# Output weights and mixed tiles loaded beside a recurrence's tail, and its sums and scales moved from VectorE to ScalarE

## The reference

```python
p = einsum('btd,de->bte', rmsnorm(x, norm_mix), w_in)          # 3584 columns: groups A, B, C
oa = stick_breaking_attention(...)                             # 4 heads x 64
ob = chunk_band_attention(...)                                 # 4 heads x 64
oc = hgrn2_scan(S0, q_c, k_c, v_c, log_f, block)               # 4 heads x 128, a gated linear recurrence
oc = rmsnorm(oc, onorm_c).reshape(B, T, W_C) * silu(gc)
mixed = concatenate([oa, ob, oc], axis=-1)                     # 1024 columns
h = x + einsum('bte,ed->btd', mixed, w_o)
u = relu(einsum('btd,df->btf', rmsnorm(h, norm_ffn), w_up))    # 4096 columns
return h + einsum('btf,fd->btd', u * u, w_down)
```

## Time and profile before

| what | us |
|---|---|
| median of 3 runs (lowest, highest) | 3034.61 (3033.84, 3037.02) |
| the profiled execution | 3033.76 |
| its span | 3031.6 |
| TensorE busy in the span | 2923.2 (96%) |
| VectorE busy | 1647.0 (54%) |
| ScalarE busy | 959.6 (32%) |
| GpSimd busy | 327.8 (11%) |

### The profile page before, as it was taken

The page is one execution under the profiler, slowest core; times in us unless marked ns, Lnnn a source line. Parts: engine busy times, 40 slices in busy tenths (PEclk is TensorE's granted clock), DMA queues, the critical chain, the costliest instruction groups (busy, mean ns, idle before and its releaser), DMA issues.

```text
span 3031.6 us, 45479 instructions
## 1 busy us (share of the span) xinstructions
PE 2923.2 (96%) x18136; PEld 2590.6 (85%) x18136; DVE 1647.0 (54%) x2293; ACT 959.6 (32%) x1639; POOL 327.8 (11%) x504
## 2 busy tenths in 40 slices
PE   7999899899999999759999999999999999999999
PEld 5788788888888999748999999889999997888887
DVE  5554454476666578843544454535444545355554
ACT  3331366455555222122222222222222222222221
POOL 2222200020001346620000000000000000000000
PEclk9999999999999999979999999999999999999999
DMA  8733332353223553332221121322211212333332
GB/s 262 254 127 122 103 89 74 124 162 106 79 86 98 161 158 120 92 137 84 70 84 56 56 83 70 125 84 70 84 56 56 84 70 100 126 125 125 125 128 100
DMA packets 285059, 327.28 MB, mean 108 GB/s; under 512 B 53644, under 2 KB 234478, under 8 KB 284850
## 3 DMA queue, kind: packets, MB, share of 16 engines
q1 hardware_dynamic: 284850, 324.38, 32.5%
HBM read 256.28 MB, written 67.78 MB: 107 GB/s over the span
## 4 chain that ended last, share of the span: by engine, by line
PE 54%; issue 1%; DVE 1%; ACT 1%; DMA 0%; SPq 0%; ACTq 0%
PE mf_psO L2194 28%; PE mf_psT L2246 22%; PE mf_psO L2246 1%; PE mf_psO L2217 1%; PE mf_psT L2180 1%; ACT mf_whi L1986 0%; DMA mf_nat<-scratch_mix 0%; PE mf_psO L2229 0%; DVE mf_acc L2147 0%; DVE mf_wlo L2060 0%; DVE mf_acc L2157 0%; ACT mf_hs L2042 0%; DVE mf_acc L2083 0%; DVE mf_hs L2089 0%; ACT mf_xhi L2001 0%
## 5 line engine op out<-in xcount | busy, mean ns | idle before, releaser
L2147 DVE TENSOR_TENSOR mf_acc<-mf_psO,mf_acc 128x1024 f32<-128x1024 f32 x256 | 313.4, 1224 | 348.0 <-PE mf_psO L2194 346.9
L2246 PE MATMUL mf_psT<-mf_xhi,mf_wlo 128*128 128x384 f32 (+1 forms) x1440 | 459.7, 319 | 0.0
L2246 PE MATMUL mf_psT<-mf_xlo,mf_whi 128*128 128x384 f32 (+1 forms) x1440 | 459.6, 319 | 0.0
L2246 PE MATMUL mf_psT<-mf_xhi,mf_whi 128*128 128x384 f32 (+1 forms) x1440 | 459.4, 319 | 0.0
L2194 PE MATMUL mf_psO<-mf_whi,mf_uhi 128*128 128x512 f32 x1024 | 401.4, 392 | 4.0 <-DVE mf_acc L2147 2.2
L2194 PE MATMUL mf_psO<-mf_whi,mf_ulo 128*128 128x512 f32 x1024 | 399.3, 390 | 0.0
L2194 PE MATMUL mf_psO<-mf_wlo,mf_uhi 128*128 128x512 f32 x1024 | 399.1, 390 | 0.0
L1986 ACT ACTIVATE mf_whi<-mf_st 128x2048 fp32r<-128x2048 f32 x108 | 202.3, 1910 | 609.9 <-PE mf_psO L2194 603.3
L2060 DVE TENSOR_TENSOR mf_wlo<-mf_st,mf_whi 128x2048 fp32r<-128x2048 f32 x108 | 243.8, 2289 | 66.4 <-ACT mf_whi L1986 66.4
L2246 PEld LDWEIGHTS mf_psT<-mf_xhi,mf_whi 128*128 128x128 f32 x1440 | 270.5, 188 | 1.6
L2246 PEld LDWEIGHTS mf_psT<-mf_xlo,mf_whi 128*128 128x128 f32 x1440 | 270.5, 188 | 1.6
(11 more groups left out here) (207 smaller groups left out, 5509.6 us busy)
## 6 DMA issues: line engine op xcount, KB each, us to landing
mf_st<-in_w_up SPq DMA_DIRECT2D x48, 1024.0 KB, 6.3
mf_st<-in_w_down SPq DMA_DIRECT2D x48, 1024.0 KB, 4.9
wst<-in_w_in SPq DMA_DIRECT2D x24, 1024.0 KB, 5.3
pj_wst<-in_w_in SPq DMA_DIRECT2D x36, 512.0 KB, 6.2
scratch_proj<-pj_ob SPq DMA_DIRECT2D x48, 256.0 KB, 2.0
mf_st<-in_w_o SPq DMA_DIRECT2D x12, 1024.0 KB, 5.4
pj_xin<-in_x_prompt SPq DMA_DIRECT2D x16, 512.0 KB, 7.2
md_qn<-scratch_proj SPq DMA_DIRECT2D x64, 128.0 KB, 2.6
```

The costliest lines, as they stand in the source:

```text
L2147: nc.vector.tensor_tensor(acc[0:r, i, :], psO[k % 2][0:r, :], acc[0:r, i, :], ALU.add).then_inc(s["o_out"], 1)
L2246: last = nc.tensor.matmul(up_psum(t, f, b, cn), wa[b4][:, w0:w0 + P], xa[:, j, c0:c0 + cn], start=j == 0 and q == 0, stop=j == KD - 1 and ...
```

## The change

1. The ring keeps its address, and `middle` puts four buffers `wo` (8 KB of each partition each, together as large as the ring) there, and `nat` (two tiles of mixed rows) where D's output buffers were. Eight steps of the plan behind the last D, SyncE waits for D's last stores, loads all of w_o into `wo`, waits for the stores of A, B and of recurrence tiles 0 and 1, and loads those two mixed tiles. The end of the block waits for these loads too.
2. `merge_and_ffn` takes these buffers over; its other buffers are placed around them, some over `wo`. The four pieces of w_o do not pass through `st` any more. In the first third, ScalarE and VectorE split the four weight pieces and tiles 0 and 1; TensorE transposes tiles 0 and 1, and tile i + 2 behind the product of tile i. SyncE issues the rows of x of tile i ahead of the mixed tile i + 2. The wait for the norm's weights moves to their first use.
3. In the recurrence ScalarE squares each head by itself with an accumulated sum and scales each head; VectorE's two steps are gone.

```diff
@@ recurrence, scalar
                 act.wait_ge(s["o_done"], n + 1)
-                nc.scalar.activation(sqo[bb][0:r, :].rearrange("p (h t) -> p h t", h=H), psO[0:r, :, :],
-                                     ACT.Square).then_inc(s["sq_ready"], 1)
+                if n >= 2:
+                    act.wait_ge(s["rsm_ready"], n - 1)
+                for h in range(H):
+                    last = nc.scalar.activation(sqo[bb][0:r, h * P:(h + 1) * P], psO[0:r, h, :], ACT.Square,
+                                                accum_out=so[bb][0:r, h:h + 1])
+                last.then_inc(s["so_ready"], 1)
+            n = tile_at(spot, OSC)
+            if n is not None:
+                r, bb = tiles[n][1], n % 2
+                act.wait_ge(s["rs_ready"], n + 1)
+                if n >= 2:
+                    act.wait_ge(stored[bb], 16 * (n // 2))
+                for h in range(H):
+                    last = nc.scalar.activation(on[bb][0:r, h * P:(h + 1) * P], psO[0:r, h, :], ACT.Copy,
+                                                scale=rs[bb][0:r, h:h + 1])
+                last.then_inc(s["osc_ready"], 1)
@@ recurrence, vector
-            dve.wait_ge(s["sq_ready"], n + 1)
-            nc.vector.tensor_reduce(so[bb][0:r, :], sqo[bb][0:r, :].rearrange("p (h t) -> p h t", h=H),
-                                    axis=AX.X, op=ALU.add).then_inc(s["so_ready"], 1)
...
-            dve.wait_ge(s["rs_ready"], n + 1)
-            if n >= 2:
-                dve.wait_ge(stored[bb], 16 * (n // 2))
-            nc.vector.tensor_tensor(on[bb][0:r, :].rearrange("p (h t) -> p h t", h=H), psO[0:r, :, :],
-                                    rs[bb][0:r, :].unsqueeze(2).to_broadcast([r, H, P]),
-                                    ALU.mult).then_inc(s["osc_ready"], 1)
@@ middle
+        raw = Map(nc, ring.at, "md_")
+        wo = [raw.sb(f"wo{i}", [P, 2 * D]) for i in range(4)]
+        nat_at = Dn.outputs_at
+        nat = Map(nc, nat_at, "md_").sb("nat", [P, 2, D])
+        next_at = max(i for i, kind in enumerate(plan) if kind == "D") + 8
...
+            def load_next():
+                Dn.wait_all(sp)
+                for i in range(4):
+                    sp.dma_start(wo[i][:, :].rearrange("p (k n) -> p k n", k=2), w_o[i * 2 * P:(i + 1) * 2 * P, :].rearrange("(k p) n -> p k n", p=P)
+                                 ).then_inc(ring.loaded[i % 2], 16)
+                B.outputs_stored(sp)
+                A.outputs_stored(sp)
+                for i in range(2):
+                    C.wait_stored(sp, i)
+                    sp.dma_start(nat[:, i, :], mix_rows[i * P:(i + 1) * P, :]).then_inc(ring.loaded[i], 16)
+
+            run(Dn.sync(sp), B.sync(sp), A.sync(sp), C.sync(sp), next_at, load_next)
+            for i in range(2):
+                sp.wait_ge(ring.loaded[i], Dn.ring_loads(i) + 16 * 3)
@@ merge_and_ffn, sync
-                sp.dma_start(nat[n % 2][0:r, :], mix[t0:t0 + r, :]).then_inc(nat_loaded[n % 2], 16)
+                if n >= 2:
+                    sp.dma_start(nat[n % 2][0:r, :], mix[t0:t0 + r, :]).then_inc(nat_loaded[n % 2], 16)
...
-            for i in range(len(THIRDS[0])):
-                load_mixed(0, i)
...
                     sp.dma_start(xin[n % 2][0:r, :], x(t0, r)).then_inc(x_loaded[n % 2], 16)
+                    if t == 0 and i + 2 < len(tiles):
+
+                        load_mixed(0, i + 2)
@@ merge_and_ffn, scalar
                 if t == 0:
-                    hi_mixed(0)
+                    for i in range(KD // FP):
+                        split(0, "o", i)
+                        if i < 2:
+                            hi(0, i, False)
                 for i in range(nt):
+                    if t == 0 and i + 2 < nt:
+                        hi(0, i + 2, False)
@@ merge_and_ffn, vector
-                for i in range(nt if t == 0 else 0):
-                    lo_mixed(0, i)
+                if t == 0:
+                    for i in range(KD // FP):
+                        split(0, "o", i)
+                        if i < 2:
+                            lo(0, i, False)
                 for i in range(nt):
+                    if t == 0 and i + 2 < nt:
+                        lo(0, i + 2, False)
@@ merge_and_ffn, tensor
-                for i in range(nt if t == 0 else 0):
+                for i in range(2 if t == 0 else 0):
                     turn(0, i, False)
                 for i in range(nt):
                     pe.wait_ge(s["lo_ready"], t_index(t, i, False) + 1)
                     out_proj(i)
+                    if t == 0 and i + 2 < nt:
+                        turn(0, i + 2, False)
                     if i >= 1:
                         turn(t, i - 1, True)
```

More of the change, by code:

```diff
@@ L706, in dense @@
     stage.wait_third = lambda eng, t: wait_stored(eng, third_end(t))
+    stage.outputs_at = outputs_at
+    stage.ring_loads = lambda i: 16 * len(range(i, len(pieces), 2))
     stage.wait_all = lambda eng: wait_stored(eng, len(units) - 1)
@@ L1291, in recurrence @@
     names = """init qp_begun qp_ready ks_ready tot_ready a_ready taken placed khT_ready khn_ready
-        o_done s_done s_out sq_ready so_ready rsm_ready rs_ready osc_ready on_ready""".split()
+        o_done s_done s_out so_ready rsm_ready rs_ready osc_ready on_ready""".split()
     s = {z: sem(z) for z in names}
@@ L1550, in vector @@
                 take(*z)
-            for step, do in ((SOUT, state_out), (RMS, out_rms), (OSC, out_scale)):
-                n = tile_at(spot, step)
-                if n is not None:
-                    do(n)
+            n = tile_at(spot, SOUT)
+            if n is not None:
+                state_out(n)
             yield
@@ L1621, in recurrence, with middle @@
     stage = Stage(len(SPOTS), sync, gpsimd, scalar, vector, tensor)
+    stage.wait_stored = lambda eng, n: eng.wait_ge(stored[n % 2], 16 * (n // 2 + 1))
     stage.load_turn = lambda n: NPOS * n - LOAD + 1 if n else 0
     return stage
-def middle(nc, ring, xhi, xlo, xt, w_in, lower_bounds, onorm, proj, tr, sources_a, sources_b, bias, sources_c, states, mix):
+def middle(nc, ring, w_o, xhi, xlo, xt, w_in, lower_bounds, onorm, proj, tr, sources_a, sources_b, bias, sources_c, states, mix):
     ctx = ExitStack()
+    mix_rows = mix
     with ctx:
@@ L1808, in order_of, with turn_order @@
             return [n - 1, *range(n - 1)] if t == LAST and p >= 0 else list(range(n))
+        def turn_order(t):
+            n = len(THIRDS[t])
+            if t:
+                return [(i, False) for i in range(n)] + [(i, True) for i in range(n)]
+            out = [(0, False), (1, False)]
+            for i in range(n + 1):
+                out += [z for z in ((i + 2, False), (i - 1, True)) if 0 <= z[0] < n]
+            return out
         def t_index(t, i, second):
-            return 2 * n0[t] + (len(THIRDS[t]) if second else 0) + i
+            return 2 * n0[t] + turn_order(t).index((i, second))
         def o_index(t, i, p):
@@ L1850, in wbuf, with landed @@
             return p if what == "o" else p % 2 + 2 * (what == "d")
+        def landed(m):
+            return wo[m] if m < KD // FP else st[m % 2]
         def piece_src(what, p):
@@ L1983, in split @@
                 m = piece(t, what, p)
-                act.wait_ge(w_loaded[m % 2], 16 * (m // 2 + 1))
+                if m >= KD // FP:
+                    act.wait_ge(w_loaded[m % 2], 16 * ((m - KD // FP) // 2 + 1))
                 wait_wbuf_free(act, t, what, p)
-                nc.scalar.activation(whi[wbuf(what, p)][:, :], st[m % 2][:, :], ACT.Copy
+                nc.scalar.activation(whi[wbuf(what, p)][:, :], landed(m)[:, :], ACT.Copy
                                      ).then_inc(s["whi_ready"], 1)
```

70 lines of the change are left out of this document (38 added, 32 removed).

## The result

The changed kernel takes **3012.38 us** (median of 4 runs, 3011.96 to 3015.89), where the one before takes 3035.52 on the same chip (4 runs, 3033.84 to 3037.02): a ratio of 0.9928, 95% interval [0.9916, 0.9939]. Forecast were 3018.0 us and a range of 3010.5 to 3024.0. The profiled execution took 3011.96 us.

A forecast was written before the change was run, and what follows sets the result against it. The entry was taken as bound by a chain of waits, no step TensorE's own limit, the lone recurrence by GpSimd's chain. 13.4 + 1.3 + 1.9 = 16.6 us off 3033.76 gave 3017.2, as median 3018.0; range 3010.5 to 3024.

The forecast's parts named there:

- Entry: Feed-forward block's start to first output product's end: 16.9 us earlier, 3.5 put off, net 13.4 us, bounds 8.5 and 14.6.
- the last gate: Entry: VectorE's low split of the fourth weight piece, forecast done at 1341.6, with 30 matmuls of the first product behind it.
- six matmuls at the low clock: First output product: of 30 matmuls behind the fourth weight piece, six at 0.43 us, the others at 0.227.
- Loads cost nothing: Beside the recurrence's tail: 5.2 MB of early loads fit before tile 12's loads are needed, by 2 us at 303 GB/s.
- The recurrence alone: Recurrence without projections: sums and scales on ScalarE save 0.2 us per tile over 6.6 tiles, 1.3 us, bounds 0 and 7.8.
- The recurrence's end: Last chain 1.0 to 1.8 us shorter, one tile earlier 0 to 0.7; together 1.9 us, bounds 1.0 and 2.5.
- the squares with their accumulator reads: Recurrence: ScalarE's four squares with accumulator reads take 1.3 to 1.85 us, so sums end 1.9 to 2.4 us earlier.
- While projections run: Recurrence beside projections, TensorE busy 39.04 of 40 us: no gain in the sum, only a possible loss, (c).
- the signs written down: First product starting about 5.5 us and ending 21 to 22 behind block start; ScalarE 2.3 us busier per tile; period 13.9.
- (a): Rival: VectorE bounded the lone recurrence; 1.2 us per tile, 6.5 more in all, about 3011.5, period near 12.9; chance 0.15.
- (b): Rival: clock stays low through the first output product, gain 11.7 us, 3022.9; a late tile 12 counted here; chance 0.15.
- (c): Rival: ScalarE becomes the narrow place while projections run, up to 3.8 us for some 8 tiles, 3048; chance 0.04.

The follow-up runs named there:

- c2: The changed kernel with 17 spare transposes on TensorE before the recurrence's last output product and 52 behind it; 3012.43 us.
- d1: The changed kernel with the 4 MB of output weights read twice in the early burst; 3021.02 us.
- c5: The changed kernel with VectorE's tile-1 low part behind the weight splits, last state stores before last row stores, and 17 plus 36 spare transposes; 3013.07 us.
- b3: The changed kernel with VectorE's low part of mixed tile 1 behind the weight splits and last state stores ahead of last mixed-row stores; 3013.33 us.

## Why the prediction was right, and where it was short

The direction and the main term hold; 5.6 us are missing, all on the side of the gain. By the steps:

- **Entry, 13.4 us forecast, 14.4 measured** (17.86 less the 3.5 put off). The row of steps came out almost to the tenth: the last gate was put 13.57 us behind the block's start and stands at 13.48 (1334.33 - 1320.85). The term that was mis-sized is "six matmuls at the low clock" behind that gate. TensorE in the first product:

```profile
1330.30 0.63 PE L2260 MATMUL mf_psO<-mf_whi,mf_xhi 128*128 128x512 f32 x1
...
1331.12 0.40 PE L2260 MATMUL mf_psO<-mf_whi,mf_xlo 128*128 128x512 f32 x1
1332.13 0.50 PE L2260 MATMUL mf_psO<-mf_whi,mf_xhi 128*128 128x512 f32 x1 [0.62 <-DVE mf_wlo L2119]
...
1334.33 0.51 PE L2260 MATMUL mf_psO<-mf_whi,mf_xhi 128*128 128x512 f32 x1 [0.54 <-DVE mf_wlo L2119]
```

  The clock is up from 1331.1 on, before the last two gates: the transposes and the first eleven matmuls had already run at the low clock, and most of what they lost lay in VectorE's shadow (c2 gains 0.3 us without it). The 30 matmuls behind the gate took 7.09 us, where 6 x 0.43 + 24 x 0.227 = 8.0 was reckoned: 0.9 of the 1.0 us. The product ended 20.6 behind the start, where 21 to 22 was written. The put-off transposes cost the forecast 3.5.
- **Loads cost nothing: right**, with GpSimd's tile 12 at its own pace (13.84 us behind tile 11) and the six reads issued between 1211.7 and 1214.8. The margin of 2 us was reckoned from 303 GB/s, where the burst moved at 415, and with no term for the held issues; d1 shows that the conclusion was safe for this burst and not for twice as much.
- **The recurrence alone, 1.3 forecast, 1.65 measured**, 0.27 us a tile for 0.2. The reading of GpSimd's chain was right and gave 0.20; the 0.07 of the scaling, which goes with the meeting of VectorE and GpSimd, I had not seen in the rows.
- **The recurrence's end, 1.9 with bounds 1.0 and 2.5; 3.70 measured**, of it 2.66 the change's own and 1.04 the clock's, which is chance: it fell later in the one profiled execution than in the other. Behind the last product it is 2.16, above the forecast 1.0 to 1.8: GpSimd's mean starts 1.20 us behind the first square instead of 3.80, 2.6 us earlier for 1.9 to 2.4, and the scaling costs 0.43 more, for 0.6 to 0.9. One tile earlier it is 0.50, within the 0 to 0.7. The mis-sized term is the squares with their accumulator reads, which took 1.12 us in all, for 1.3 to 1.85, since they overlap: ScalarE from first square to last read, and the scaling.

```profile
1312.62 0.27 ACT L1476 ACTIVATE md_rcsqo<-md_psO 32x128 f32<-32x128 f32 x1 [3.34 <-PE md_psO L1617]
...
1313.55 0.19 ACT L1476 ACTIVATION_READ_ACCUMULATOR md_rcsqo<-md_psO 32x1 f32 x1
...
1315.12 1.11 ACT L1486 ACTIVATE md_rcon<-md_psO,md_rcrs 32x128 f32<-32x128 f32 x4 [1.39 <-POOL md_rcrs L1436]
```

  The four scalings took 1.11 to 1.14 us; the Trainium skill's figures (ScalarE: Activation LUTs, "What ACT_TABLE_LOAD costs") had given an estimate of 1.27 (summed again, 1.26). Its rule that multiplications belong on VectorE (the same page, "Rules for kernel authors") holds for the bare chain at the recurrence's end, 0.67 us, and where the sums stay on VectorE, 0.2 us over all; with the sums moved it fails, and the kernel gains 1.1.
- **While projections run, nothing forecast, 1.66 measured.** This is the step that failed outright, in a prediction whose time lies within its range: the sum had no term here, since TensorE is busy 39 of 40 us and I looked in this stretch only for a loss. The 3.1 us of waits for VectorE were there to be asked for.
- Summed: 1.0 + 0.35 + 0.76 + 1.04 + 1.66 = 4.8. Two parts are chance between two executions, 0.17 in the arrival at tile 2 and 0.24 in the rest; another 0.4 is that before's profiled execution was taken as 0.85 below its median where after's lies 0.42 below: 5.6.

Of the signs written down, the first product began 5.44 us behind the block's start (5.5 forecast) and the period is 13.84 us (13.9), but ScalarE is busier by 28.0 us over 17 tiles, 1.65 a tile and not 2.3.

Of the rivals, (a) would have shown a period near 12.9 and is out at 13.84. (b) is out: the clock rose within the product (at 1331.1), and the entry with the transposes at the high clock, c2's, is only 0.3 us shorter. (c) is out: TensorE's waits while projections run became shorter.

## What to carry to other kernels

- Where a block opens with loads, take both the loads and the order of its first work: here taking away the loads alone, in the old order, would have left 30.3 of 38.4 us, and both together leave 20.6. Once no load is left, count the in-order engines that split or convert: moving one 1.2 us operation out of VectorE's row gave 0.6 us, where a high clock gave 0.3; behind that move the clock gave 0.8.
- A stretch in which TensorE is 97% busy still has waits worth asking for, and two delays of the same engine can hide each other: moved singly the two operations gave 0.35 and 0.55 us, together 1.66, most of the excess in a single period of tiles.
- Differences of 1 us between kernels whose runs spread by 3 are read from anchors inside the trace, and a stage that holds a fall of TensorE's clock is compared with that product's length taken off.

## What the runs showed of the hardware that was not expected

- **The clock fell while TensorE did not stop.** In c5 the granted clock was 1.00 from 1315.5 to 1316.0, 0.50 from 1316.5 to 1323.0 and 1.00 again from 1323.5, with TensorE busy throughout, from the 17 transposes at 1311.04 on but for 0.33 us. In c2 it was 0.50 from 1314.0 to 1317.0, with TensorE as busy, and 1.00 again from 1317.5. What ran were 128x128 transposes and the last tile's products of 32 rows; in both the clock came back while nothing but spare transposes ran. The Trainium skill (TensorE: Matmul & The Clock Gate, "What's actually happening") says that the throttled state is the default and activity releases it; these rows show a fall in the midst of activity, which that sentence alone does not explain. With the 17 transposes ahead of it the last product was high from end to end in all three kernels that had them; in the eleven others in none.
- **When the clock falls differs between executions of the same code**, by 2 us or more, enough for 1.4 us in the length of one product (3.09 to 4.47).
- **SyncE itself is held** for 4.44 us on one issue (`md_rck`) behind the burst of 5.2 MB, and for 5.65 on one (`md_rcf`) behind that of 9.4 MB, where such an issue otherwise takes 0.5 us (1205.09 in the changed kernel); the issues behind it in its order go out later by that much.
- **The way to tile 2** took 1043.5 to 1049.7 us in the same code. In the traces of after and b3, the first and the last to get there, the granted clock between 550 and 600 us was 0.97 and 0.86 and the matmuls there 244 and 217. But in before it was 0.90 with 237, and before reached tile 2 at 1043.70, only 0.17 behind after. So that stretch is not the whole of it, and why one execution falls lower than another no run here shows.
